# SBUF layout of a fused two-block network: scalars first, then a pad, so that the streamed buffers begin on other addresses

## The reference

```
first_block: h = concat(meta (16), x (512))
             h = h + hybrid_mixer(rmsnorm(h))     # gated delta rule + stick-breaking attention,
                                                  # gated, merged @ w_out
             h = h + swiglu(rmsnorm(h))           # 1024 -> 2 x 2816 -> 1024
second:      (scale, shift, gate) = silu(c) @ ada_w[l] + ada_b[l]     # 6 x 1024 a layer, 2 layers
             layer 0: grouped-query attention, then conv_ffn
             layer 1: hyena (long convolution by DFT), then conv_ffn  # 1024 -> 2 x 2816 -> 1024
             out = rmsnorm(h)
```

## Time and profile before

| | |
|---|---|
| median of 3 runs | 2914.71 us (2913.64 to 2916.36) |
| profiled execution: span | 2914.1 us |
| PE busy / DVE / ACT / POOL | 2801.0 (96%) / 1311.9 (45%) / 709.7 (24%) / 1605.7 (55%) us |
| mean granted TensorE clock | 0.979 |
| DMA | 260.22 MB, mean 89 GB/s |

### The profile page before, as it was taken

How to read it: one execution, slowest core, us unless ns; L and a number is a source line. 1 busy time by engine, 2 the same in 40 slices (tenths; PEclk the granted TensorE clock), 3 DMA queues, 4 the chain that set the end, 5 groups by cost and what they waited for, 6 DMA issues and landing times.

```text
span 2914.1 us, 39863 instructions
## 1 busy us (share of the span) xinstructions
PE 2801.0 (96%) x15611; PEld 2263.8 (78%) x15611; DVE 1311.9 (45%) x1932; ACT 709.7 (24%) x1094; POOL 1605.7 (55%) x1569
## 2 busy tenths in 40 slices
PE   8999989999999999999999999999999898999999
PEld 7998888799678787888865578888777455788887
DVE  6677562311710575333346733331276678433311
ACT  3275223532620002110026621110111222211100
POOL 7653124655076665666651157767675534676664
PEclk9999999999999999999999999999999999999999
DMA  4211001222022565565520023332322000233331
GB/s 129 87 59 35 2 2 45 86 77 83 1 87 88 184 204 167 180 190 194 187 95 22 30 58 101 102 96 96 102 87 91 25 12 15 87 92 97 107 100 68
DMA packets 292585, 260.22 MB, mean 89 GB/s; under 512 B 6617, under 2 KB 264390, under 8 KB 292156
## 3 DMA queue, kind: packets, MB, share of 16 engines
q1 hardware_dynamic: 289492, 250.83, 27.6%
q0 software_dynamic: 2416, 6.34, 0.7%
q10 hardware_dynamic: 504, 0.66, 0.1%
HBM read 255.72 MB, written 2.10 MB: 88 GB/s over the span
## 4 chain that ended last, share of the span: by engine, by line
PE 84%; DVE 6%; issue 4%; DVEq 2%; ACT 2%; POOL 1%; DMA 1%; POOLq 0%; ACTq 0%; SPq 0%
PE ps L532 23%; PE ps L534 23%; PE ps L533 23%; PE ps L1746 1%; PE ps L1766 1%; PE ps L1672 1%; PE ps L1609 1%; PE ps L1589 1%; PE ps L1599 1%; PE ps L1354 1%; PE ps L1333 1%; PE ps L935 1%; PE ps L1361 1%; PE ps L1265 1%; DVE cv L2330 0%
## 5 line engine op out<-in xcount | busy, mean ns | idle before, releaser
L821 POOL CAST spl<-raw 128x512 fp32r<-128x512 f32 (+1 forms) x352 | 246.8, 701 | 655.2 <-PE ps L534 518.3
L532 PE MATMUL ps<-HSH,spl 128*128 128x512 f32 x1344 | 536.8, 399 | 19.9 <-DVE HSL L743 16.0
L533 PE MATMUL ps<-HSL,spl 128*128 128x512 f32 x1344 | 528.5, 393 | 0.0
L823 POOL TENSOR_TENSOR spl<-raw,spl 128x512 fp32r<-128x512 f32 (+1 forms) x352 | 497.5, 1413 | 56.1 <-issue 6.2
L534 PE MATMUL ps<-HSH,spl 128*128 128x512 f32 x1344 | 528.1, 393 | 0.0
L827 POOL TENSOR_TENSOR spl<-raw,spl 128x512 fp32r<-128x512 f32 (+1 forms) x352 | 479.8, 1363 | 51.5 <-issue 1.3
L532 PE MATMUL ps<-HNH,spl 128*128 128x264 f32 (+1 forms) x1152 | 365.8, 318 | 3.4 <-DVE HNL L713 2.9
L533 PE MATMUL ps<-HNL,spl 128*128 128x264 f32 (+1 forms) x1152 | 356.9, 310 | 0.0
L534 PE MATMUL ps<-HNH,spl 128*128 128x264 f32 (+1 forms) x1152 | 355.7, 309 | 0.0
L825 POOL CAST spl<-raw 128x512 fp32r<-128x512 f32 (+1 forms) x352 | 232.7, 661 | 209.6 <-PE ps L534 207.6
L532 PEld LDWEIGHTS ps<-HSH,spl 128*128 128x128 f32 x1344 | 255.2, 190 | 95.0 <-issue 38.2
(11 more groups left out here) (459 smaller groups left out, 4415.3 us busy)
## 6 DMA issues: line engine op xcount, KB each, us to landing
adw<-in_ada_w SPq DMA_DIRECT2D x96, 512.0 KB, 5.6
raw<-in_w_in SPq DMA_DIRECT2D x44, 1024.0 KB, 5.2
raw<-in_ffn_w_up SPq DMA_DIRECT2D x88, 512.0 KB, 5.0
raw<-in_w_ffn_in SPq DMA_DIRECT2D x44, 512.0 KB, 5.1
raw<-in_ffn_w_down SPq DMA_DIRECT2D x16, 1408.0 KB, 6.2
raw<-in_hy_w_in SPq DMA_DIRECT2D x12, 1024.0 KB, 5.1
raw<-in_w_ffn_out SPq DMA_DIRECT2D x8, 1408.0 KB, 6.7
raw<-in_w_branch_dn SPq DMA_DIRECT2D x8, 1024.0 KB, 5.0
```

Of the source, the lines that this page charges most:

```text
L532: pe.matmul(dst, w[0], x[0], start=first, stop=False)
L533: pe.matmul(dst, w[0], x[1], start=False, stop=False)
L821: pool.tensor_copy(hi[:, first, :], w[:, first, :])
L823: pool.tensor_tensor(lo[:, first, :], w[:, first, :], hi[:, first, :], ALU.subtract).then_inc(split_first, 1)
```

## The change

`tiny`, `gsc` and `csil` (48 words) move to the front, a pad brings the next address to a multiple of 128 words (512 bytes), and `raw` begins there. `mod` (96 words) is dropped: the modulation sums are written over the bias rows `ada_b` in `pcol`, which nobody reads afterwards. Three places that were counted from word 0 are now counted from `raw_at`.

```
+        LINE = 128
+        tiny = fresh("tiny", 8)
+        eps, zero = tiny[:, 0:1], tiny[:, 1:2]
+        gsc = fresh("gsc", 2, 2, KD)
+        csil = fresh("csil", KD)
+        here[0] += -(top[0] // 4 + here[0]) % LINE
+        raw_at = here[0]
         raw = fresh("raw", 2, SLOT)
...
         ones = fresh("ones", P)
-        tiny = fresh("tiny", 8)
-        eps, zero = tiny[:, 0:1], tiny[:, 1:2]
-        mod = fresh("mod", 2, 6 * KD)
-        gsc = fresh("gsc", 2, 2, KD)
-        csil = fresh("csil", KD)
...
+        mod = cols("ada_b", 0, 2 * 6 * KD).rearrange("p (l n) -> p l n", l=2)
...
-        here[0] = SLOT + 2 * NT * SEQ // 2
+        here[0] = raw_at + SLOT + 2 * NT * SEQ // 2
...
-        t_fwd = at("t_fwd", [2, NT, SEQ // 2], hy_in.slot(10) * SLOT)
-        t_inv = at("t_inv", [2, 2, SEQ], hy_in.slot(11) * SLOT)
+        t_fwd = at("t_fwd", [2, NT, SEQ // 2], raw_at + hy_in.slot(10) * SLOT)
+        t_inv = at("t_inv", [2, 2, SEQ], raw_at + hy_in.slot(11) * SLOT)
...
-            dve.tensor_tensor(mod[:, :, :].rearrange("p l n -> p (l n)"), ps[:, 4, 0:ADA], cols("ada_b", 0, ADA), ALU.add)
+            dve.tensor_tensor(cols("ada_b", 0, ADA), ps[:, 4, 0:ADA], cols("ada_b", 0, ADA), ALU.add)
```

## The result

The changed kernel takes 2898.25 us (median of 4 runs, 2895.56 to 2900.69), the kernel before beside it 2914.18 us (4 runs, 2913.40 to 2916.36): 0.9946 of the time, 95% interval 0.9933 to 0.9959. The forecast was 2907.1 us, range 2901 to 2915. The sign was right; the gain is 15.9 us where 7.6 were worked out, and the time lies under the range.

What follows compares the result with a forecast made beforehand. The prediction took PE's pace on the matmuls of `products` as the bound. Its terms, 3.5 + 2.5 + 1.3 + 0.3 = 7.6 us, took 2914.1 to 2906.5 us; the runs' median, 0.6 us higher, gave 2907.1, range 2901 to 2915.

Steps and rivals of the forecast that it cites:

- What bounds the kernel, and that the pace of a product depends on its buffer: Products on PE: PE 84% of the chain; full-clock steps of 512 columns take 226.7 to 233.3 ns depending on the streamed buffer.
- `AFH`/`AFL` 3.5 us, `OGH`, `ZH`, `MGH` 1.3 us: Upper tensors, moved onto multiples of 128 bytes: 1584 and 576 matmuls each gain 2.2 ns, 3.5 and 1.3 us.
- `VOH`/`VOL` 2.5 us: Four-piece stream: 384 matmuls go from 233.3 to 226.7 ns, a price for each piece's beginning; 2.5 us, lower bound 0.
- `OSH`/`OSL` 0.3 us: 192 matmuls, `OSL` aligned afterwards only in every second row: between 0 and 1.0 us, taken as 0.3.
- `HSH` and `HNH` at 0 us: Lower tensors, moved by 384 bytes: `HSH` keeps 226.7 ns and `HNH` 231.5 ns, so 0 us.
- the unit is 128 bytes: Streamed fp32r operands: the pace depends on where each row begins modulo 128 bytes, a multiple being quickest.
- The rest at 0 us: Modulation sums, scalars at the front, plain float32 matmuls, DVE, ACT and POOL operands, and DMA: 0 us each.
- Sum of the addresses, 7.6 us: Whole kernel: 3.5 + 2.5 + 1.3 + 0.3 = 7.6 us off the profiled execution, 2914.1 to 2906.5.
- The rule against it: Trainium skill's SBUF page, 16-byte lines: every address was already on a line, so the sum would be 0.
- the last sentence of the rivals: Whole kernel: a stage starting sooner moves against the clock's halving; size taken as 2.7 us, the spread of three runs.
- much faster: Streamed operands: unit 256 bytes, a start on it best, 1.5 ns per matmul, 10 us more: 2897 us; chance 0.08.
- Slower, the unit is 256 bytes: Streamed operands: its first half is the bad place; `HSH` loses 8.9 us, upper tensors win nothing: 2923.6 us; chance 0.08.

Runs made afterwards that it cites:

- pace_2: Separate program of fp32r matmuls, no reference work, with more stream-to-weights distances, four pieces and 16 weight columns: 226.7 ns at 256 bytes, 228.9 at 320, 236.8 at 4.
- spl_apart: Changed kernel with 32 words more between `spl` and `H`, so streams lie 128 bytes from the weights modulo 256: 2938.35 us, 1.0087 of the kernel before.
- pace: Separate program, no reference work: groups of 36 fp32r matmuls, moving only the stream or the weights; 226.7 ns with the stream 0 beyond, 228.9 at 64, 233.3 at 128.
- upper_only: Kernel before with only the upper tensors moved by -192 bytes, `raw` to `HSL` left in place: 2920.02 us, 1.0018 of the kernel before.
- all_64: Changed kernel with 16 words more ahead of `raw`, so nothing streamed begins on a multiple of 128 bytes: 2899.58 us, 0.9946 of the kernel before.
- before_moved_1h: Kernel before with one small hyena-stage matmul issued once more in full and once with half its columns, 1.29 us, no address changed: 2906.9 us.
- after_moved_3: Changed kernel with one small hyena-stage matmul issued three more times, 2.6 us, no address changed: 2907.65 us.
- rows_aligned: Changed kernel with the weights of three GEMMs stored so each piece has its row's place modulo 256 bytes: 2904.39 us, 0.9954 of the kernel before.

## Why the prediction was wrong in size

- **What bounds the kernel, and that the pace of a product depends on its buffer.** Right: PE 84% of the chain after as before, and each buffer's step is a property of the addresses.
- **`AFH`/`AFL` 3.5 us, `OGH`, `ZH`, `MGH` 1.3 us.** Right: subtracted matmul by matmul where both profiled executions run at full clock, the steps of `AFH` and `AFL` give 3.35 us (0.96 to 1.2 in each of the three stages) and the other three with their low parts 1.1 us; `MGH` still has a mean of 227.6 ns, the others 226.8 to 226.9.
- **`VOH`/`VOL` 2.5 us.** Right in size: the same subtraction gives 2.55 us, and the steps are 226.7 ns. The reason given, a price for each piece's beginning, is not borne out: four pieces 64 bytes beyond cost what one does in `pace_2`.
- **`OSH`/`OSL` 0.3 us.** A mean of 232.1 ns after and 231.9 before: nothing came of it.
- **`HSH` and `HNH` at 0 us.** Nearly right in value: `HNH` gave 0.0 us, and `HSH` with `HSL` cost 0.9 us (a mean of 227.1 ns after and 226.9 before), which stays unexplained. The step "they stood on multiples of 128 and stand on multiples of 128, if that is the unit" was wrong as a rule: it was enough only because `spl` moved by the same 384 bytes. `spl_apart` has all of them on multiples of 128 and is 36 to 40 us slower. The sentence "the unit is 128 bytes" falls with `pace`, `upper_only` and `all_64`; what replaces it is the distance to the weights modulo 256.
- **The rest at 0 us.** Plain float32 matmuls and all other work of PE at full clock changed by 0.04 us in sum. The first matmul of the execution, which waits for `xt`, starts 0.35 us earlier; the other two transfers of the earlier trace rows were not looked at by themselves.
- **Sum of the addresses, 7.6 us.** The measured terms are 3.35 + 2.55 + 1.1 + 0.0 = 7.0 us, and 6.1 with what `HSH` cost. Whole runs bear it out to within a few us, by pairs in which the hyena stage behaves alike: `before_moved_1h` less its 1.3 us against the changed kernel, 2906.9 - 2898.25 = 8.7 us (7.4 when each is held against the kernel before beside it); the kernel before against `after_moved_3` less its 2.6 us, 2914.45 - 2907.65 = 6.8 us.
- **The rule against it**, by which every start on a multiple of 16 bytes costs the same and the sum is 0: it falls with `pace_2`, where 16 bytes beyond took 231.8 ns and 0 beyond 226.7.
- **The step that failed** is the last sentence of the rivals: a stage that starts sooner moves against the moments at which the clock is halved, "the three runs differ by 2.7 us already, which I take as the size of that". That term was sized from executions of one program, which all have the same gaps in the hyena stage, and left out of the sum and nearly out of the range. It measures 7.6 us in that stage here: 5.1 us of clock and 2.4 us of waits. In the latter 4.5 us for `AS` go and 1.5 us come back in other waits; part of that idle time lies in halved stretches, so the two don't add up exactly. The stretch behind the filter gap is what sets the wait for `AS` off. Nothing in the prediction looked at how a halved stretch changes which engine is ahead of which.
- **The rival "much faster" (2897)** named nearly the right time for a wrong reason, and that is luck: `HSH` did not get faster, where it wanted 1.5 ns. **"Slower, the unit is 256 bytes"** had the right period, but measured from 0 instead of from the weights.

Still open: how often one kernel falls into either group, as each was profiled once and `rows_aligned` shows both clumps; why `VOH` cost 233.3 ns before and 228.9 in `pace_2` at the same distance; by what rule rows that wander cost 231.5; and why the changed kernel in all of its layouts and shifts came into the quiet part at the second gap, while the kernel before and its shifts came into the other. The runs show that the place of the gap sorts all 17 traces, and that a shift of 1.3 us turns it; what brings each family of kernels to its place, stretch by stretch, they don't.

## What to carry to other kernels

For fp32r products at full clock with 128 weight columns and rows that all begin at one place, choose the distance between the streamed rows and the weights, modulo 256 bytes, and not the alignment of either: 0 gave 226.7 ns for 512 columns, other distances up to 236.8. When a change shifts a TensorE-bound kernel by a few us, a stage with idle gaps of 1 to 4 us may answer by more than the shift, as one did here; test a gain by moving the stage alone before crediting it to the edit. Where a short wait has VectorE operations on two SBUF inputs ahead of it, look at what GpSimd does at that moment.

## What the runs showed of the hardware that was not expected

- An fp32r matmul of 512 columns takes 226.7 ns with stream and weights 0 or 256 bytes apart, 228.9 at 64 and 320, 230.0 at 48, 231.8 at 16, 233.3 at 128, 192 and 224, 234.3 at 160, 236.8 at 4; with 16 weight columns only 2.2 ns lie between 0 and 128. With the streamed buffers 128 bytes from the kernel's weights instead of 0, the kernel takes 36 us more by the profiled executions and 40 by the medians, of 2898.
- The halved stretches of an execution (a granted clock of 0.5, which is 1.2 of 2.4 GHz) began at multiples of 3.41 us from one another in all 17 traces of the network and lasted 3.4 to 13.7 us. In these traces the same idle gap of 1.97 us was followed by one in each of the nine in which it began 0.30 to 1.35 us behind such a multiple, and by none in the eight in which it began 1.48 to 1.93 us behind.
- A VectorE tensor_tensor of 128x512 with both inputs in SBUF takes 0.69 us, and 1.58 to 1.75 us when it starts while GpSimd runs its own; GpSimd's own goes from 1.27 to 1.71 us.
